# Half of the key projection and the first FFN 2 round on raw, pivot-shifted x in a one-core decoder step

## The chip, the cores and the metric

One core of a Trainium2 chip runs the whole kernel in one launch. The metric is device time in microseconds; lower is better. TensorE is called PE, VectorE DVE, ScalarE ACT, GpSimd POOL and SyncE SP, as in the profile.

## The reference

One layer for 512 prompt tokens and 32 sample tokens (8 sequences of 4), in float32:

```python
x = layer_norm(ALPHA * x + 0.5 * swiglu(x, ffn1_w_gu, ffn1_w_down), ln_g[0], ln_b[0])
qa, ka, va, qr, kr, vr, gr, ga, gb = split(x @ w_in)
oa = diff_post(diff_attention(qa, ka, va))          # paged cache for the sample group
ob = ret_post(retention(qr, kr, vr), gr)
m = sigmoid(ga) * (oa @ w_pa) + sigmoid(gb) * (ob @ w_pb)
x = layer_norm(ALPHA * x + m @ w_o, ln_g[1], ln_b[1])
x = layer_norm(ALPHA * x + 0.5 * swiglu(x, ffn2_w_gu, ffn2_w_down), ln_g[2], ln_b[2])
```

`layer_norm` subtracts the mean over the 1,024 channels, divides by the root of variance + eps, multiplies by a gain and adds a bias, both per channel. `swiglu(x)` is `(silu(a) * u) @ w_down` with `a, u` the halves of `x @ w_gu` (2 x 2,816 columns). The keys `ka` are also an output.

## The kernel before

**Layout.** x stands with channels on partitions: `xT` is 8 channel tiles (KD = 8, index k) of 128 channels x 544 tokens (512 prompt, then 32 sample). Every gemm is a sum of three float32r products, so each operand is split in a high and a low part: `xh`, `xl` for x, `w_hi_t`, `w_lo_t` for weights, `hh`, `hl` for the FFN's hidden tiles, `mh`, `ml` for the merged branches. `gemm` (L289 on) makes one output tile of 128 columns x 544 tokens in two PSUM banks: for each k three products of two halves of 272 tokens, 48 matmuls for 8 k. PSUM has eight banks, so four such tiles.

**Weights.** Chunks of 256 columns (two output tiles) are loaded by SP into one of two `w_raw` buffers, cast by ACT to `w_hi_t` (`split_hi`, once PE is done with the chunk two before) and subtracted by DVE to `w_lo_t` (`split_lo`). PE waits for `lo_split`; SP loads the next chunk into the buffer once the split of the last one there is done.

**Order of work.** Nothing is planned at run time: each engine runs its list of classes in the order in which the blocks at the end of `build` call their `pe_part`, `act_part`, `dve_part` and `pool_part`, and engines meet through semaphores. Around the change the order is: FFN 1 (11 rounds of up chunks, then 12 down chunks), the first channel norm `ln1`, key projection `pk`, value projection, query projection; and much later the output projection `out_proj`, the second channel norm `ln2`, FFN 2 and the last norm `ln3`, which is of another kind and not touched.

**The channel norm** (L571 on). DVE adds each residual tile to `x_sum` as it comes (`dve_add`). After the last one PE sums over partitions with a matrix of ones (L608), DVE centres the eight tiles (L639), ACT squares each (L627) and PE accumulates the squares' sums (L614); ACT takes the root (L629), DVE the reciprocal (L642); then per tile DVE scales (L646), ACT adds the bias twice, into `xh` and `xT` (L633, L634), and DVE makes `xl` (L651). The first gemm behind the norm, tile 0 of `pk` or of FFN 2's first round, waits for each k's `xl` (`ready`).

**Key projection** (`Project`, L660 on). Eight tiles on two pairs of banks. ACT evicts a tile to `turned` (L728), PE transposes it to token rows after the next tile's gemm (`turn`, L699 and L701), DVE copies the rows to `k_nat` (L742, L744), POOL copies the tile to `kaT` (L751).

**FFN** (L315 on). A round makes two tiles of a and two of u in all eight banks: ACT applies silu (L373), DVE multiplies (L394), ACT and DVE split the product. The down projection adds its tiles into `xT` (L413); `out_proj` does the same at L1813.

## Time and profile before

| | |
|---|---|
| median of three timed runs | 1946.93 us (1946.41 to 1950.22) |
| profiled execution: span from its first to its last instruction | 1943.7 us |
| median less that span | 3.2 us |
| PE busy in the span | 1804.9 us, 93% |
| DVE, ACT, POOL busy | 778.9, 667.4, 85.2 us |
| mean granted PE clock | 0.968 of full |

The profile gives the profiled execution's time as its span; what lies around the span is seen only as the distance to the timed runs. The page's 40 slices of 48.6 us show PE at nine tenths or more nearly everywhere; lower are the start, the stretch of the attentions, and single slices near 440 and 1500 us.

### The profile page before, as it was taken

Reading aid. Unit: us, or ns where it says so; the run is one execution under the profiler, and the core shown is the slowest. Engines: PE = TensorE matmul, PEld = TensorE weight load, DVE = VectorE, ACT = ScalarE, POOL = GpSimd, SP = SyncE. Lnnn points to the kernel's source line nnn. Section 1 sums busy time; section 2 is a strip of 40 time slices with the busy share of each in tenths; the row PEclk is TensorE's granted clock in tenths of the full one; section 3 lists DMA queues with packets and bytes.
Section 4 is the critical chain, followed back from the end, with each engine's and each line's share of the span. In section 5 each row is a group of like instructions: output and inputs, shape, how many; then the busy total and the mean of one; then the engine's idle time right before and its main releaser. Section 6 shows DMA issues by size and latency. Waiting matters only on the chain.

```text
span 1943.7 us, 33105 instructions
## 1 busy us (share of the span) xinstructions
PE 1804.9 (93%) x13247; PEld 1699.9 (87%) x13247; DVE 778.9 (40%) x1081; ACT 667.4 (34%) x899; POOL 85.2 (4%) x113
## 2 busy tenths in 40 slices
PE   6999999998997768999989999999999899999996
PEld 5999999987997537878768999869998799999996
DVE  2333332234223875756663223344345433333123
ACT  3333331124223555666563222124322433332111
POOL 0000000000002420000000000110000000000002
PEclk9999999999997998999989999999999999999998
DMA  4222222230440015767752232062223022222221
GB/s 142 91 90 91 89 84 82 81 108 22 133 133 23 1 51 176 273 228 249 242 169 91 87 98 84 17 215 66 91 91 100 22 86 87 89 90 84 92 97 46
DMA packets 146659, 203.75 MB, mean 105 GB/s; under 512 B 5538, under 2 KB 127330, under 8 KB 146594
## 3 DMA queue, kind: packets, MB, share of 16 engines
q1 hardware_dynamic: 145442, 198.35, 31.4%
q0 software_dynamic: 1152, 4.46, 0.6%
q8 instruction: 49, 0.80, 0.2%
q14 instruction: 16, 0.13, 0.0%
HBM read 191.39 MB, written 11.40 MB: 104 GB/s over the span
## 4 chain that ended last, share of the span: by engine, by line
PE 88%; DVE 4%; ACT 4%; issue 2%; DMA 0%; SPq 0%; POOL 0%; ACTq 0%; POOLq 0%; DVEq 0%
PE ps L297 68%; PE ps L1201 4%; PE ps L1232 3%; PE ps L1187 2%; PE ps L974 1%; PE ps L988 1%; PE ps L614 1%; PE ps L1624 1%; PE ps L1211 1%; PE ps L1616 1%; PE ps L1248 1%; PE ps L699 1%; PE ps L1198 1%; ACT aT L1069 1%; PE ps L981 0%
## 5 line engine op out<-in xcount | busy, mean ns | idle before, releaser
L297 PE MATMUL ps<-xh,w_hi_t 128*128 128x272 f32 x2432 | 510.1, 291 | 25.3 <-DVE xl L651 18.3
L297 PE MATMUL ps<-xh,w_lo_t 128*128 128x272 f32 x2432 | 505.9, 290 | 0.0
L297 PE MATMUL ps<-xl,w_hi_t 128*128 128x272 f32 x2432 | 504.2, 289 | 0.0
L283 DVE TENSOR_TENSOR w_lo_t<-w_raw,w_hi_t 128x2048 fp32r<-128x2048 f32 (+1 forms) x112 | 252.4, 2254 | 519.2 <-ACT w_hi_t L279 519.2
L297 PEld LDWEIGHTS ps<-xh,w_hi_t 128*128 128x128 f32 x2432 | 385.0, 190 | 30.2 <-issue 20.7
L297 PEld LDWEIGHTS ps<-xl,w_hi_t 128*128 128x128 f32 x2432 | 385.1, 190 | 0.0
L297 PEld LDWEIGHTS ps<-xh,w_lo_t 128*128 128x128 f32 x2432 | 382.4, 190 | 0.0
L279 ACT CAST w_hi_t<-w_raw 128x2048 fp32r<-128x2048 f32 (+1 forms) x112 | 209.9, 1874 | 276.5 <-PE ps L297 276.5
L297 PE MATMUL ps<-hh,w_lo_t 128*128 128x272 f32 x704 | 145.7, 288 | 0.0
L297 PE MATMUL ps<-hh,w_hi_t 128*128 128x272 f32 x704 | 145.5, 288 | 0.0
L297 PE MATMUL ps<-hl,w_hi_t 128*128 128x272 f32 x704 | 145.1, 288 | 0.0
L297 PEld LDWEIGHTS ps<-hh,w_hi_t 128*128 128x128 f32 x704 | 110.7, 188 | 0.0
L297 PEld LDWEIGHTS ps<-hl,w_hi_t 128*128 128x128 f32 x704 | 110.6, 189 | 0.0
L297 PEld LDWEIGHTS ps<-hh,w_lo_t 128*128 128x128 f32 x704 | 109.9, 189 | 0.0
L1303 DVE TENSOR_TENSOR kt_lo<-ps,kt_hi 128x512 fp32r<-128x512 f32 x128 | 82.5, 685 | 57.3 <-ACT kt_hi L1302 57.1
L377 ACT CAST hh<-prod 128x544 f32 x44 | 28.6, 649 | 216.0 <-DVE prod L394 216.0
L1302 ACT CAST kt_hi<-ps 128x512 fp32r<-128x512 f32 x128 | 70.3, 587 | 66.9 <-PE ps L1187 66.7
L1187 PE MATMUL ps<-ident,k_page 128*128 128x128 f32 x512 | 74.8, 285 | 14.1 <-DVE kt_lo L1303 12.4
L1324 DVE TENSOR_TENSOR vp_lo<-v_page,vp_hi 128x1024 fp32r<-128x1024 f32 x64 | 76.4, 1222 | 19.3 <-ACT vp_hi L1320 18.9
L1187 PEld LDWEIGHTS ps<-ident,k_page 128*128 128x128 f32 x512 | 57.5, 144 | 29.1 <-DVE kt_lo L1303 12.8
L394 DVE TENSOR_TENSOR prod<-ps,gated 128x544 f32<-128x544 f32 x44 | 31.9, 725 | 108.2 <-PE ps L297 108.2
L1201 PE MATMUL ps<-kt_hi,q_stat 128*128 128x256 f32 x256 | 71.9, 314 | 0.0
(245 smaller groups left out, 2107.0 us busy)
## 6 DMA issues: line engine op xcount, KB each, us to landing
w_raw<-in_ffn_w_gu_dram SPq DMA_DIRECT2D x44, 1024.0 KB, 5.1
w_raw<-in_w_in_dram SPq DMA_DIRECT2D x32, 1024.0 KB, 5.7
k_page<-in_cache_k_dram SPq DMA_DIRECT2D x64, 512.0 KB, 4.8
v_page<-in_cache_v_dram SPq DMA_DIRECT2D x64, 512.0 KB, 4.6
w_raw<-in_ffn_w_down_dram SPq DMA_DIRECT2D x16, 1024.0 KB, 5.1
w_raw<-in_ffn_w_down_dram SPq DMA_DIRECT2D x8, 768.0 KB, 4.7
w_raw<-in_w_branch_a_dram SPq DMA_DIRECT2D x4, 1024.0 KB, 5.2
st_in<-in_state_ret_dram SPq DMA_DIRECT2D x8, 512.0 KB, 5.0
```

What stands on the lines that cost most here:

```text
L279: nc.scalar.copy(w_hi_t[:, j, 0:nk], w_raw[:, j, 0:nk]).then_inc(hi_split, 1)
L283: nc.vector.tensor_tensor(w_lo_t[:, j, 0:nk], w_raw[:, j, 0:nk], w_hi_t[:, j, 0:nk].bitcast(F32), ALU.subtract).then_inc(lo_split, 1)
L297: mm = nc.tensor.matmul(ps[:, bank + half, 0:HALF], w[:, j, k, w_cols], m[:, k0 + k, half * HALF:half * HALF + HALF], start=start and k == ...
L377: nc.scalar.copy(hh[:, bass.ds(2 * i + n, 1)], prod[:, n:n + 1]).then_inc(self.h_hi, 1)
L394: nc.vector.tensor_tensor(halves(prod[:, n]), banks(4 + 2 * n), halves(gated[:, n]), ALU.mult).then_inc(self.prod_done, 1)
L614: mm = nc.tensor.matmul(ps[:, 2 + a, 0:HALF], ones[:], x_sq[:, k % 2, a * HALF:a * HALF + HALF], start=k == 0, stop=k == KD - 1)
L1187: mm = nc.tensor.transpose(ps[:, half, h * P:h * P + P], k_page[:, g % 4, (4 * half + h) * P:(4 * half + h) * P + P], ident[:])
L1201: mm = nc.tensor.matmul(dst, q_stat[:, P * h:P * h + P], kt[:, q % 2, h], start=False, stop=h == HA - 1 and kt is kt_lo)
L1232: mm = nc.tensor.matmul(ps[:, 6 + half, :], pT[:, g], v[:, g % 2, 512 * half:512 * half + 512], start=g == 0 and v is vp_hi, stop=False)
L1302: return nc.scalar.copy(at_hi, src)
L1303: return nc.vector.tensor_tensor(at_lo, src, at_hi.bitcast(F32), ALU.subtract)
L1324: nc.vector.tensor_tensor(vp_lo[:, g % 2], v_page[:, g % 4], vp_hi[:, g % 2].bitcast(F32), ALU.subtract).then_inc(self.v_lo, 1)
```

## The change

In both channel norms the gemm behind the norm starts on x that is not yet normalised. With gain g, bias b, mean m and 1/root r per token, `W'((x - m) r g + b) = r (W'(x g) - m W'g) + W'b`. So `xh`, `xl` first hold x times gain, and two more columns (544 becomes 546) hold -g and b; their gemm gives `-W'g` and `W'b` beside the tile. An eviction then computes `(ps + m * fold0) * r` on DVE (`dve_fix`) and adds `fold1` on ACT or in the product. To keep x small, a pivot (the mean over the first two channel tiles) is subtracted early from all eight tiles of `xT` (`dve_pivot`, 8 additions on DVE), while the producer's gemms still run.

- Raw x feeds tiles 0 to 3 of `pk` (all eight came from normalised x) and the whole first round of FFN 2 (four tiles). From tile 4 of `pk` and the second round on, gemms read normalised x.
- Statistics: ACT squares each residual tile, POOL adds the squares into `x_ssq`, and one PE pair per sum gives both sums in the middle of the first raw tile, before k = 5 (`pe_stats`). The variance is the mean square less the squared mean.
- Normalised x: POOL subtracts the mean from the eight tiles, DVE scales, ACT adds the bias and casts to `xh`, DVE makes `xl`; `xh[k]` is overwritten once PE is done with k of the last raw tile (`freed`).
- FFN's down loops, `out_proj` and FFN 2's first round are written out instead of looped. `x_rs`, `x_mu`, `x_msq` and `x_fix` lie in the place of `hh`.

The diff's core (the old bodies of `ChannelNorm` and the key tiles' use of `Project`, printed above, go):

```diff
         xT = at("xT", 49152, [KD, T])
-        xh = at("xh", 66560, [KD, T], F32R)
-        xl = at("xl", 83968, [KD, T], F32R)
-        A = 101376
+        xh = at("xh", 66560, [KD, T + 2], F32R)
+        xl = at("xl", 84032, [KD, T + 2], F32R)
+        A = 101504
...
-        def gemm(bank, j, n, nk, mh_, ml_, k0=0, start=True, stop=True, tile_ready=None):
+        def gemm(bank, j, n, nk, mh_, ml_, k0=0, start=True, stop=True, tile_ready=None, extra=0, freed=None,
+                 between=None):
 
             for k in range(nk):
+                if between and k == 5:
+                    between()
                 if tile_ready:
                     tile_ready(k)
                 w_cols = slice(n * P, n * P + P)
                 for pas, (w, m) in enumerate(((w_hi_t, mh_), (w_hi_t, ml_), (w_lo_t, mh_))):
                     for half in range(2):
-                        mm = nc.tensor.matmul(ps[:, bank + half, 0:HALF], w[:, j, k, w_cols],
-                                              m[:, k0 + k, half * HALF:half * HALF + HALF],
+                        cols = HALF + extra * half
+                        mm = nc.tensor.matmul(ps[:, bank + half, 0:cols], w[:, j, k, w_cols],
+                                              m[:, k0 + k, half * HALF:half * HALF + cols],
                                               start=start and k == 0 and pas == 0,
                                               stop=stop and k == nk - 1 and pas == 2)
+                if freed and k < nk - 1:
+                    mm.then_inc(freed, 1)
             mm.then_inc(gemm_done, 1)
...
+            def pe_stats(self, pe):
+                pe.wait_ge(self.summed, KD * self.i + KD)
+                for a in range(2):
+                    nc.tensor.matmul(ps[:, 4 + a, 0:HALF], ones[:], x_sum[:, a * HALF:a * HALF + HALF],
+                                     start=True, stop=True)
+                pe.wait_ge(self.ssq, KD * self.i + KD)
+                for a in range(2):
+                    mm = nc.tensor.matmul(ps[:, 6 + a, 0:HALF], ones[:], x_ssq[:, a * HALF:a * HALF + HALF],
+                                          start=True, stop=True)
+                mm.then_inc(self.spread, 1)
+
...
+            def act_take(self, act, k, resid, r0):
+                act.wait_ge(resid, r0 + k + 5)
+                act.wait_ge(self.shifted, KD * self.i + KD)
+                act.wait_ge(self.ssq, KD * self.i + k)
+                nc.scalar.activation(x_sq[:], xT[:, k], ACT.Square).then_inc(self.squared, 1)
+                nc.scalar.mul(xh[:, k, 0:T], xT[:, k], self.gain(k)).then_inc(self.raw_hi, 1)
+
+            def act_stats(self, act):
+                act.wait_ge(self.spread, 2 * self.i + 2)
+                nc.scalar.activation(halves(x_msq[:]), banks(4), ACT.Square, scale=1.0 / D).then_inc(self.moment, 1)
+                nc.scalar.mul(halves(x_mu[:]), banks(4), 1.0 / D).then_inc(self.moment, 1)
+                act.wait_ge(self.scale_set, 2 * self.i + 1)
+                nc.scalar.activation(x_rs[:], x_rs[:], ACT.Sqrt, bias=guard[:]).then_inc(self.moment, 1)
+
...
+            def act_high(self, act, k, c):
+                act.wait_ge(self.y, KD * self.i + k + 1)
+                if k < KD - 1:
+                    act.wait_ge(self.freed, (KD - 1) * self.i + k + 1)
+                else:
+                    tile_done(act, c, 1)
+                nc.scalar.copy(xh[:, k, 0:T], xT[:, k]).then_inc(self.y_hi, 1)
+
...
+            def dve_pivot(self, dve):
+                dve.wait_ge(self.kept, 3 * self.i + 3)
+                dve.wait_ge(self.summed, KD * self.i + 1)
+                nc.vector.scalar_tensor_tensor(x_sum[:], x_nc[:], float(self.PIVOT), x_sum[:], ALU.mult, ALU.add
+                                               ).then_inc(self.summed, 1)
+                for k in range(KD):
+                    nc.vector.tensor_tensor(xT[:, k], xT[:, k], x_nc[:], ALU.add).then_inc(self.shifted, 1)
+
...
+                dve.wait_ge(self.shifted, KD * self.i + KD)
+                dve.wait_ge(self.summed, KD * self.i + k)
+                nc.vector.tensor_tensor(x_sum[:], x_sum[:], xT[:, k], ALU.add).then_inc(self.summed, 1)
+                self.dve_raw_low(dve, k)
+
+            def dve_raw_low(self, dve, k):
+                dve.wait_ge(self.raw_hi, KD * self.i + k + 1)
+                nc.vector.scalar_tensor_tensor(xl[:, k, 0:T], xT[:, k], self.gain(k), xh[:, k, 0:T].bitcast(F32),
+                                               ALU.mult, ALU.subtract).then_inc(self.raw_lo, 1)
+
+            def dve_fix(self, dve, u, c, n, bank):
+
+                s = u % 2
+                f = self.f0 + u
+                tile_done(dve, c, n)
+                if u >= 2:
+                    self.fix_free(dve, u)
+                nc.vector.tensor_copy(fold[:, 2 * s:2 * s + 2], ps[:, bank + 1, HALF:HALF + 2]).then_inc(self.fixed, 1)
+                dve.wait_ge(self.fixed, 3 * f + 1)
+                dve.wait_ge(self.moment, 3 * self.i + 2)
+                nc.vector.scalar_tensor_tensor(halves(x_fix[:, s]), halves(x_mu[:]), fold[:, 2 * s:2 * s + 1], banks(bank),
+                                               ALU.mult, ALU.add).then_inc(self.fixed, 1)
+                dve.wait_ge(self.fixed, 3 * f + 2)
+                nc.vector.tensor_tensor(x_fix[:, s], x_fix[:, s], x_rs[:], ALU.mult).then_inc(self.fixed, 1)
+
+            def dve_scale(self, dve, k):
+                dve.wait_ge(self.centered, KD * self.i + k + 1)
+                nc.vector.scalar_tensor_tensor(xT[:, k], xT[:, k], self.gain(k), x_rs[:], ALU.mult, ALU.mult
+                                               ).then_inc(self.scaled, 1)
+
+            def dve_low(self, dve, k):
+                dve.wait_ge(self.y_hi, KD * self.i + k + 1)
+                nc.vector.tensor_tensor(xl[:, k, 0:T], xT[:, k], xh[:, k, 0:T].bitcast(F32), ALU.subtract
+                                        ).then_inc(self.x_lo, 1)
+
+            def pool_part(self, pool):
+                for k in range(KD):
+                    pool.wait_ge(self.squared, KD * self.i + k + 1)
+                    if k == 0:
+                        nc.gpsimd.tensor_copy(x_ssq[:], x_sq[:]).then_inc(self.ssq, 1)
+                    else:
+                        pool.wait_ge(self.ssq, KD * self.i + k)
+                        nc.gpsimd.tensor_tensor(x_ssq[:], x_ssq[:], x_sq[:], ALU.add).then_inc(self.ssq, 1)
+                pool.wait_ge(self.moment, 3 * self.i + 2)
+                pool.wait_ge(self.raw_lo, (KD + 2) * (self.i + 1))
+                for k in range(KD):
+                    nc.gpsimd.tensor_tensor(xT[:, k], xT[:, k], x_mu[:], ALU.subtract).then_inc(self.centered, 1)
...
+        class NormedProject(Project):
+            RAW = 4
...
+            def pe_part(self, pe):
+                for u in range(self.tiles):
+                    if u % 2 == 0:
+                        chunk_ready(pe, self.c + u // 2)
+                    pe.wait_ge(self.taken, self.t0 + u + 1)
+                    ready = {0: lambda k: self.norm.raw_ready(pe, k), self.RAW: lambda k: self.norm.ready(pe, k)}.get(u)
+                    gemm(2 * (u % 2), (u // 2) % 2, u % 2, KD, xh, xl, tile_ready=ready, extra=2 if u < self.RAW else 0,
+                         freed=self.norm.freed if u == self.RAW - 1 else None,
+                         between=None if u else lambda: self.norm.pe_stats(pe))
+                    if u > 0:
+                        self.turn(pe, u - 1)
+
+            def act_part(self, act):
+                self.norm.act_stats(act)
+                for u in range(self.tiles):
+                    if u == self.RAW - 1:
+                        for k in range(KD):
+                            self.norm.act_high(act, k, self.c + u // 2)
+                    s = u % 2
+                    if u < self.RAW:
+                        act.wait_ge(self.norm.fixed, 3 * (self.norm.f0 + u) + 3)
+                    else:
+                        tile_done(act, self.c + u // 2, s)
+                    act.wait_ge(self.rows, self.r0 + u + 1)
+                    act.wait_ge(self.kept, self.k0 + u + 1)
+                    if u < self.RAW:
+                        nc.scalar.activation(self.stage[:, s], x_fix[:, s], ACT.Identity, bias=fold[:, 2 * s + 1:2 * s + 2]
+                                             ).then_inc(self.taken, 1)
+                    else:
+                        nc.scalar.copy(halves(self.stage[:, s]), banks(2 * s)).then_inc(self.taken, 1)
+                    if u % 2 == 1:
+                        c = self.c + u // 2 + 2
+                        split_hi(act, c, c // 2, (u // 2) % 2)
+                    if u < self.RAW - 1:
+                        for k in range(3 * u, min(3 * u + 3, KD)):
+                            self.norm.act_bias(act, k)
...
+                self.norm.dve_stats(dve)
+                for u in range(self.tiles):
+                    if u == self.RAW - 1:
+                        for k in range(KD):
+                            self.norm.dve_low(dve, k)
+                    if u < self.RAW:
+                        self.norm.dve_fix(dve, u, self.c + u // 2, u % 2, 2 * (u % 2))
+                    if u:
+                        keep(u - 1)
+                    if u % 2 == 1:
+                        split_lo(dve, self.c + u // 2 + 2, (u // 2) % 2)
+                    if u < self.RAW - 1:
+                        for k in range(3 * u, min(3 * u + 3, KD)):
+                            self.norm.dve_scale(dve, k)
+                keep(self.tiles - 1)
...
+                if folded:
                     for n in range(2):
+                        folded.dve_fix(dve, n, c, n, 2 * n)
+                split_lo(dve, c + 2 * i + 2, 0)
+                if folded:
+                    for k in range(KD):
+                        folded.dve_scale(dve, k)
+                for n in range(2):
+                    if folded:
+                        folded.dve_fix(dve, 2 + n, c + 1, n, 4 + 2 * n)
+                    else:
                         tile_done(dve, c + 2 * i + 1, n)
...
+                    if folded and n == 0:
+                        for k in range(KD):
+                            folded.dve_low(dve, k)
+                split_lo(dve, c + 2 * i + 3, 1)
...
+                for k in range(KD):
+                    c = self.c + k // 2
+                    tile_done(dve, c, k % 2)
+                    if k > 2:
+                        ln2.dve_shifted(dve)
+                    nc.vector.scalar_tensor_tensor(halves(xT[:, k]), banks(2 * (k % 4)), 1.0 / ALPHA, halves(xT[:, k]),
+                                                   ALU.mult, ALU.add).then_inc(self.resid, 1)
+                    if k == 2:
+                        dve.wait_ge(self.resid, k + 5)
+                        ln2.dve_pivot(dve)
+                        ln2.dve_raw_low(dve, 0)
+                        ln2.dve_raw_low(dve, 1)
+                    ln2.dve_take(dve, k, self.resid, 0)
+                    if k % 2 == 1:
+                        split_lo(dve, c + 2, k // 2 % 2)
+                ln2.dve_stats(dve)
```

In FFN 1's last down chunk ACT casts the next weight chunk and then takes tiles 6 and 7 (`act_take`); DVE's order there and at two other places is shown below. How instructions move:

DVE, from the last residual tiles of FFN 1 on, before (`L413` residual, `L603` running sum, `L283` weight split, `L639` centring, `L646` scale):

```order
L413 SCALAR_TENSOR_TENSOR xT<-ps,xT 128x544 x2
L603 TENSOR_TENSOR x_sum<-x_sum,xT 128x544 x2
L283 TENSOR_TENSOR w_lo_t<-w_raw,w_hi_t 128x2048
L639 SCALAR_TENSOR_TENSOR xT<-ps,xT 128x544 x8
L642 RECIPROCAL x_rs<-x_rs 128x544
L646 SCALAR_TENSOR_TENSOR xT<-xT,ln_cols,x_rs 128x544 x2
L651 TENSOR_TENSOR xl<-xT,xh 128x544
```

The same place now (`L796` sum, `L801` raw split, `L806` variance, `L819` to `L825` the fix of tile 0, `L829` scale):

```order
L493 SCALAR_TENSOR_TENSOR xT<-ps,xT 128x544 x2
L796 TENSOR_TENSOR x_sum<-x_sum,xT 128x544
L801 SCALAR_TENSOR_TENSOR xl<-xT,ln_cols,xh 128x544
L796 TENSOR_TENSOR x_sum<-x_sum,xT 128x544
L801 SCALAR_TENSOR_TENSOR xl<-xT,ln_cols,xh 128x544
L289 TENSOR_TENSOR w_lo_t<-w_raw,w_hi_t 128x2048
L806 SCALAR_TENSOR_TENSOR x_rs<-ps,x_msq 128x544
L809 RECIPROCAL x_rs<-x_rs 128x544
L819 COPY small<-ps 128x2
L822 SCALAR_TENSOR_TENSOR x_fix<-x_mu,small,ps 128x544
L825 TENSOR_TENSOR x_fix<-x_fix,x_rs 128x544
L829 SCALAR_TENSOR_TENSOR xT<-xT,ln_cols,x_rs 128x544 x3
```

The raw splits stand between the sums and the weight split moved behind them; the reciprocal is followed by a tile's fix before the first scale.

PE, between the last down gemm and the first key tile, before:

```order
L297 MATMUL ps<-hl,w_hi_t 128x272 x2
L297 MATMUL ps<-hh,w_lo_t 128x272 x2
L355 REGISTER_ALU
L355 COMPARE_AND_BRANCH
L608 MATMUL ps<-x_sum,ones 128x272 x2
L614 MATMUL ps<-x_sq,ones 128x272 x16
L297 MATMUL ps<-xh,w_hi_t 128x272 x2
L297 MATMUL ps<-xl,w_hi_t 128x272 x2
```

PE inside the first key tile now, from its channel 4 to its channel 5:

```order
L307 MATMUL ps<-xl,w_hi_t 128x272
L307 MATMUL ps<-xl,w_hi_t 128x274
L307 MATMUL ps<-xh,w_lo_t 128x272
L307 MATMUL ps<-xh,w_lo_t 128x274
L716 MATMUL ps<-x_sum,ones 128x272 x2
L720 MATMUL ps<-x_ssq,ones 128x272 x2
L307 MATMUL ps<-xh,w_hi_t 128x272
L307 MATMUL ps<-xh,w_hi_t 128x274
```

The sums moved from ahead of the first tile into it, and the 16 square-sum matmuls became two.

POOL, its first work of the kernel, before (copies of evicted key tiles):

```order
L2087 UNCONDITIONAL_BRANCH
L748 UNCONDITIONAL_BRANCH
L748 ISA
L751 ISA
L751 COPY kaT<-turned 128x544
```

And now, the squares' sums and the eight subtractions ahead of the same copies:

```order
L2361 UNCONDITIONAL_BRANCH
L841 COPY x_ssq<-x_sq 128x544
L844 ISA
L844 TENSOR_TENSOR x_ssq<-x_ssq,x_sq 128x544 x7
L848 TENSOR_TENSOR xT<-xT,x_mu 128x544 x8
L938 UNCONDITIONAL_BRANCH
L938 ISA
L941 ISA
L941 COPY kaT<-turned 128x544
```

The key copies stand behind sixteen operations that wait for ACT and DVE.

## Rows read from the trace of the kernel before

**Rows 1.** The page's chain that ended last: shares of the span by engine.

```profile
PE 88%; DVE 4%; ACT 4%; issue 2%; DMA 0%; SPq 0%; POOL 0%; ACTq 0%; POOLq 0%; DVEq 0%
```

**Rows 2.** Windows: stretch, length; busy (count) of PE, PEld, DVE, ACT, POOL; clock; DMA.

```profile
426.40:460.00 33.60, 19.88 (x79) 15.45 (x79) 24.08 (x29) 20.15 (x28) 0.00 (x0) 0.80 0.11 34
460.00:500.00 40.00, 40.00 (x323) 39.94 (x324) 11.26 (x13) 9.21 (x10) 3.85 (x6) 1.00 0.20 58
1496.50:1530.00 33.50, 20.46 (x84) 15.28 (x84) 23.53 (x28) 20.16 (x28) 0.00 (x0) 0.80 0.10 32
```

**Rows 3.** Timeline, first norm: start, length, engine, line, operation, [idle before <-releaser].

```profile
425.72 0.41 PE L297 MATMUL ps<-hl,w_hi_t 128*128 128x272 f32 x2
...
425.98 0.41 PE L297 MATMUL ps<-hh,w_lo_t 128*128 128x272 f32 x2
...
428.67 1.19 PE L608 MATMUL ps<-x_sum,ones 128*128 128x272 f32 x4 [2.28 <-DVE x_sum L603]
...
430.73 5.13 DVE L639 SCALAR_TENSOR_TENSOR xT<-ps,xT 128x544 f32<-128x544 f32 x8
...
450.03 0.79 PE L297 MATMUL ps<-xh,w_hi_t 128*128 128x272 f32 x2 [7.49 <-DVE xl L651]
...
460.75 0.42 PE L297 MATMUL ps<-xh,w_hi_t 128*128 128x272 f32 x2
```

**Rows 4.** Chain in order of time, key projection: start, length, what.

```profile
480.61 6.01 PE ps L297 x48
...
487.16 6.01 PE ps L297 x48
```

**Rows 5.** Timeline, second norm, TensorE.

```profile
1496.20 0.41 PE L297 MATMUL ps<-mh,w_lo_t 128*128 128x272 f32 x2
...
1530.15 0.41 PE L297 MATMUL ps<-xh,w_hi_t 128*128 128x272 f32 x2
```

**Rows 6.** Groups of VectorE by line and form: busy, mean ns, idle before.

```profile
L283 DVE TENSOR_TENSOR w_lo_t<-w_raw,w_hi_t 128x2048 fp32r<-128x2048 f32 x104 | 238.4, 2292 | 448.2 <-ACT w_hi_t L279 448.2
...
L646 DVE SCALAR_TENSOR_TENSOR xT<-xT,ln_cols,x_rs 128x544 f32<-128x544 f32 x16 | 12.3, 779 | 0.1
...
L642 DVE RECIPROCAL x_rs<-x_rs 128x544 f32<-128x544 f32 x2 | 7.1, 3553 | 14.3 <-ACT x_rs L629 14.3
```

**Rows 7.** Groups of ScalarE by line and form.

```profile
L279 ACT CAST w_hi_t<-w_raw 128x2048 fp32r<-128x2048 f32 x104 | 198.0, 1904 | 198.2 <-PE ps L297 198.2
...
L633 ACT ACTIVATE xh<-xT,ln_cols 128x544 fp32r<-128x544 f32 x16 | 12.0, 748 | 9.9 <-DVE xT L646 9.9
...
L627 ACT ACTIVATE x_sq<-xT 128x544 f32<-128x544 f32 x16 | 10.5, 657 | 11.6 <-PE ps L614 8.5 <-DVE xT L639 3.1
```

**Rows 8.** Groups of GpSimd by line and form.

```profile
L568 POOL TENSOR_TENSOR xn<-xn,ln_bias 128x1024 f32<-128x1024 f32 x4 | 9.4, 2345 | 639.8 <-ACT xn L508 639.8
...
L1691 POOL TENSOR_TENSOR qx<-qrT,cross 128x512 f32<-128x512 f32 x3 | 3.8, 1269 | 6.2 <-PE ps L1587 3.8 <-PE ps L1584 2.4
```

**Rows 9.** Timeline, start of the attention, VectorE and GpSimd.

```profile
610.57 2.29 DVE L283 TENSOR_TENSOR w_lo_t<-w_raw,w_hi_t 128x2048 fp32r<-128x2048 f32 x1 [9.72 <-ACT w_hi_t L279]
...
610.95 2.17 POOL L958 TENSOR_TENSOR bias<-dist,small 128x128 f32<-128x128 f32 x1 [1.16 <-DVEq L1101]
...
614.08 0.28 DVE L1020 CUSTOM_DVE_ANT_0 s_sb<-ps,bias 128x128 f32<-128x128 f32 x1
...
615.02 0.39 POOL L958 TENSOR_TENSOR bias<-dist,small 128x128 f32<-128x128 f32 x1
```

**Rows 10.** Windows behind the two idle stretches; columns as above, clock in the eighth.

```profile
450.00:452.00 2.00, 1.97 (x9) 2.00 (x10) 1.91 (x3) 1.79 (x4) 0.00 (x0) 0.50 0.00 0
...
454.00:456.00 2.00, 1.52 (x11) 1.29 (x10) 1.87 (x4) 2.00 (x4) 0.00 (x0) 0.94 0.00 0
1498.40:1500.50 2.10, 1.91 (x4) 0.96 (x4) 1.92 (x1) 1.63 (x3) 0.00 (x0) 0.57 0.00 0
```

**Rows 11.** The page's costliest group: busy, mean ns of one, idle before.

```profile
L297 PE MATMUL ps<-xh,w_hi_t 128*128 128x272 f32 x2432 | 510.1, 291 | 25.3 <-DVE xl L651 18.3
```

More of the change, by code:

```diff
@@ L379, in act_part @@
+            def act_part(self, act, folded=None, norm=None):
+                c = self.c
+                if folded:
+                    self.act_up(act, 0, folded)
+                with act.Fori(1 if folded else 0, KF // 2) as i:
+                    self.act_up(act, i)
                 c += FFN_UP
+                if norm:
+                    norm.act_columns(act)
                 for q in range(2):
@@ L384, in act_part @@
                             split_hi(act, c + nxt, (c + nxt) // 2, m % 2, 6 if m % 3 == 0 else KD)
-            def dve_part(self, dve, norm=None):
+                        if norm and q == 0 and m == 3:
+                            norm.act_pivot(act)
+                            for k in range(2):
+                                norm.act_take(act, k, self.resid, self.r0)
+                        if norm and m % 3 == 2 and (q, m) != (0, 2):
+                            for k in (4 * q + 2 * (m // 3), 4 * q + 2 * (m // 3) + 1):
+                                norm.act_take(act, k, self.resid, self.r0)
@@ L609, in pe_part @@
                                           start=True, stop=True)
-                mm.then_inc(self.mean, 1)
-                for k in range(KD):
-                    pe.wait_ge(self.squared, KD * self.i + k + 1)
-                    for a in range(2):
-                        mm = nc.tensor.matmul(ps[:, 2 + a, 0:HALF], ones[:], x_sq[:, k % 2, a * HALF:a * HALF + HALF],
-                                              start=k == 0, stop=k == KD - 1)
-                    mm.then_inc(self.sq_used, 1)
@@ L2044, in _ @@
             pe.wait_ge(cols_set, 1)
[L2045 to L2047 removed]
+            ffn1.pe_part(pe, norm=ln1)
+            pk.pe_part(pe)
             pv.pe_part(pe, before=pk)
```

328 lines of the change are left out of this document (198 added, 130 removed).

## Prediction

> **What bounds the kernel now.** I read the chain of waits first: 88% of it is TensorE (PE), so time is won only where PE stands or works in vain [rows 1]. Then the windows, for where that is: in an ordinary stretch PE is busy all the time (40.00 of 40.00 us), but in the two stretches that hold the channel layer norms it is busy for 19.88 of 33.60 and 20.46 of 33.50 us, and much of that is norm work, at a mean clock of 0.80 [rows 2]. Then the timeline, for what those stretches cost. At the first norm the last pair of FFN 1 matmuls starts at 425.98 and the second key tile at 460.75 [rows 3]. A pair starts every 0.25 us and a tile of 48 matmuls takes 6.02 [rows 4], so between these two points only 0.25 + 6.02 are gemm: 34.77 - 6.27 = **28.5 us** are lost. At the second norm the same two points are 1496.20 and 1530.15 [rows 5]: 33.95 - 6.27 = **27.7 us**. Together 56.2 us, 2.9% of the span of 1943.7. That is all there is to win, and the change must give some of it back.
>
> **What it removes.** The chain sum - mean - eight centrings - eight squares - square root - reciprocal - scale - split no longer stands between the last residual tile and the first matmul. The raw tiles of channels 0 to 5 are split while the producer's gemms still run; PE goes on with them at once. The eight square-sum pairs on PE vanish too, but they lie inside the 56.2 us.
>
> **What it adds on PE.** Per norm: one pair of ones-matmuls for the pivot and two for the statistics. The pair of today takes 1.19 us to its end [rows 3]; an end stands 0.16 behind the next start (0.41 against 0.25 [rows 3, 4]), so I take 1.03. Six pairs: **6.2 us**, all in PE's own queue. The two more columns on half of the matmuls of eight tiles are 2 in 272 of 0.125 us, under 0.2 us in all: left out.
>
> **What it adds on VectorE (DVE), ScalarE (ACT) and GpSimd (POOL).** Durations of 128x544 operations: DVE 0.72, next start after 0.64 (eight in 5.13 [rows 3]); scale or split of raw x with a gain column 0.78, weight split 2.29, reciprocal 3.55 [rows 6]; ACT square 0.66, cast with gain 0.75, weight cast 1.90 [rows 7]. POOL's two-input operation has no row of this size: 512 columns take 1.27, 1,024 take 2.35 [rows 8], so a line through both gives 1.34 for 544. A key-tile fix is three DVE operations that wait for one another: 0.2 + 0.8 + 0.8, about 1.8.
>
> One row pattern decides the sum. A POOL operation that takes 0.39 alone took 2.17 when it was issued 0.38 us behind a weight split on DVE, and ended 0.26 behind it; a DVE operation with one operand in PSUM took its usual 0.28 while POOL ran [rows 9]. I read this as: a DVE instruction with both inputs in SBUF and a POOL instruction hold each other up, whole instruction by whole instruction. The new kernel puts sixteen POOL operations per norm beside just such DVE work: the squares' sum beside raw splits, the eight subtractions (10.7 us in a row) beside fix, scale and weight split.
>
> **First norm, step by step** (us from the last FFN 1 matmul; every engine works in the order of its code):
> - PE does channels 0 to 4 of tile 0 until 3.8, then must have the full sum. DVE takes channel 7's residual (0.2), the sum of channel 6 (0.8), then the raw split of 6. That needs ACT, which first casts a weight chunk (to 2.1), squares (to 2.8) and casts (to 3.5); and POOL adds square 6 until 4.1. So the last sum is ready at 5.6, square sums 0.3 later: **2.2 idle**.
> - Statistics, variance behind a weight split (9.8 on), root, reciprocal until 14.9, fix of tile 0 held once by POOL: evicted at 17.9. PE finished tile 1 at 16.0 and waits to transpose tile 0: **1.9**.
> - DVE's scale 0 to 2 each stand behind one subtraction, so the fix of tile 1 is late: **1.2**. Tile 2's fix stands behind the weight split and scale 3 to 5: **2.1**.
> - Scale 6 and 7, their biases, then the first normalised split: ready at 38.6, PE free at 34.9: **3.7**. After that a split each 0.66 keeps ahead of PE's 0.75 per channel.
> - Tile 3's fix stands behind all eight splits: **0.9**. From there on the spacing is 6.56 as before [rows 4].
> Idle: 12.0 us.
>
> **Second norm** (us from the first out-projection matmul): pivot sum on PE at 18.1, negated mean 19.8, eight shifts until 25.7, then raw splits 0 to 3 in turn with POOL's additions; ACT's weight cast stands behind them (34.6), DVE's split ends at 38.9 where PE wanted it at 37.1: **1.9**. The statistics cost no wait here, as residuals come every 6 us. In the first FFN 2 round the fixes, the weight split and eight scales end at 78.1, then fix 2, the product, its cast, and only then the normalised splits: first at 82.8, where PE is free at 76.9: **5.9**. Idle: 7.8 us.
>
> **The clock.** [...] Four microseconds at half clock lose about 1.8 of work. I charge it twice, behind the 3.7 and the 5.9: **3.6 us**.
>
> **Sum.** 12.0 + 7.8 + 6.2 + 3.6 = 29.6 us stay; 56.2 - 29.6 = 26.6 are won. The sum is made against a profile whose span is 1943.7; the median of the runs shown, 1946.93, stands 3.2 above it, and I keep that distance: 1946.9 - 26.6 = **1920**. Hidden at no cost: the pivot's eight shifts in FFN 1's down projection (5.9 us of DVE, beside a chunk of 9 to 12 us whose weight split has some 6 to spare), the new columns (cut while that stage begins), POOL's shifts of its key copies. If that cover went, a weight split would be late and PE would wait for it, as I count for the out projection. Loads follow the weight splits on SP's queue and shift with them by 2 us at most, with a chunk's time to spare. The PE loops that are written out cost nothing: the key tiles are written out today and run at 6.02 us [rows 4].
>
> [...]
>
> **Rivals.**
> - *POOL and DVE hardly meet.* For: the episode is one, and POOL's other rows keep their length. Against: that episode has both sides of it. Without any hold the same count gives 5.8 + 5.6 of idle: 11.4 + 6.2 + 3.6 = 21.2 stay, 35.0 won, **1912**; 1908 if the clock does not fall either. Chance 0.20.
> - *A heavier POOL or more waits.* At 1.8 us per POOL operation idle is 15.6 + 13.3 and the time 1929; at 2.35 (the row of 1,024 columns, the upper bound) 1941. For: the squares' sum adds in place, which no row does at this size. Against: the rows of 1.27 hardly scatter. Chance 0.20 for 1925 to 1942.
> - *Slower: the subtractions on POOL set the order.* Everything normalised hangs on them, one after another. Above 2.6 us each the idle exceeds 46 us and the gain is gone; at 3.5 it is 31 + 39 and the time about 1970. Nothing in [rows 8] is near. The same sign would come from the new row length of xh and xl, 546 columns instead of 544, if it slowed the reads: no row shows such a stride, so its cost lies between nothing and unknown; 3 times 2,432 matmuls read them [rows 11], 7.3 us per nanosecond each, so 3.6 ns (of 125) would eat the gain. I take nothing, as the rows of hh and xh run alike. Chance 0.04.
> - *It does not do what it says:* raw tiles might still wait for the statistics. They don't by the code: only channels 5 to 7 of the first tile stand behind them. 0.01.
>
> **How the numbers follow.** Forecast 0.55 (1914 to 1925), rivals 0.20, 0.20, 0.05. The range of 1907 to 1932 takes in the forecast, the first rival and the nearer half of the second. What a measurement of this kernel can tell from no change is about 0.2%, 4 us: faster 0.93 (all but the far end of the second rival and the last two), same 0.03, slower 0.04.
>
> **What would show it.** Of the 56 us lost at the two norms about 30 should be left; the stats pair should start about 5.6 us behind the last FFN 1 matmul; PE should wait for splits of normalised x by about 4 and 6 us, clock 0.5 after it; POOL's subtractions should stretch beyond 1.34 where DVE scales, and DVE's scales beyond 0.78. Right, but for other reasons: idle of 11 us and unstretched rows. Wrong: subtractions above 2 us, gemms of xh slower than 6.02 per tile, or late weight splits in the down projection.

## The result and the profile after

The changed kernel takes 1933.84 us (median of 4 runs, 1932.99 to 1937.74) against 1948.58 for the kernel before in the same comparison (1946.41 to 1951.81): a ratio of 0.9923, 95% interval 0.9906 to 0.994. The medians differ by 14.7 us; the interval of the ratio makes that 11.7 to 18.3. It is faster, as forecast, but by about half of the 26.6 us, and 1934 lies above the range. A second comparison gave 1933.52 against 1948.56 and 0.9925 (0.9906 to 0.9944). The profiled execution has a span of 1935.7 and a time of 1937.74, the longest of its four runs.

The chain of waits on the page of the changed kernel, which answers to [rows 1]:

```profile
PE 85%; DVE 6%; ACT 5%; issue 3%; DMA 0%; SPq 0%; POOL 0%; ACTq 0%; POOLq 0%; DVEq 0%
```

TensorE still sets the end. Now the stretch that held the first norm, for TensorE, in order of time (start, length, engine, line, operation, idle before with its releaser); it answers to [rows 3]:

```profile
431.84 0.41 PE L307 MATMUL ps<-hh,w_lo_t 128*128 128x272 f32 x2
432.09 0.42 PE L307 MATMUL ps<-xh,w_hi_t 128*128 128x272 f32 x2
...
437.53 1.18 PE L716 MATMUL ps<-x_sum,ones 128*128 128x272 f32 x4 [1.45 <-DVE x_sum L796]
438.72 1.19 PE L720 MATMUL ps<-x_ssq,ones 128*128 128x272 f32 x4
...
449.39 0.66 PE L889 MATMUL ps<-ident,turned 128*128 128x128 f32 x4 [1.10 <-ACT turned L984]
...
456.43 0.66 PE L889 MATMUL ps<-ident,turned 128*128 128x128 f32 x4 [0.17 <-ACT turned L984]
...
465.07 0.66 PE L889 MATMUL ps<-ident,turned 128*128 128x128 f32 x4 [1.78 <-ACT turned L984]
...
468.63 0.79 PE L307 MATMUL ps<-xh,w_hi_t 128*128 128x272 f32 x2 [2.79 <-DVE xl L834]
```

The first key tile starts 0.25 us behind the last FFN 1 matmul, where it stood 24 us behind it before. What is left of the gap lies in five waits: for the full sum (1.45), for three evicted tiles at their transposition (1.10, 0.17, 1.78) and for normalised xl ahead of tile 4 (2.79). The groups of TensorE's waits around the second norm (what waited, for whom, us in total, times, longest):

```profile
PE ps L307 <- DVE xl L834: 4.9, 1, 4.9
PE ps L307 <- DVE w_lo_t L289: 1.6, 1, 1.6
```

From the last FFN 1 matmul to the eviction of the eighth key tile the kernel before needed 80.5 us and this one 65.5. From the last out-projection matmul to the end it was 447.5 and is 432.0. These are 15.0 and 15.5 us won, so the mechanism works. The evictions of the eighth key tile, before and after (start, length, engine, line, operation); they stand 80.50 us behind 425.98 of [rows 3] and 65.53 behind 431.84 above:

```profile
506.48 0.62 ACT L728 ACTIVATE turned<-ps 128x544 f32<-128x544 f32 x1 [5.94 <-PE ps L297]
```

```profile
497.37 0.61 ACT L987 COPY turned<-ps 128x544 f32<-128x544 f32 x1 [6.02 <-PE ps L307]
```

What ate into it is seen outside the norms. The chain in order of time, for key and value tiles of the changed kernel (start, length, what, matmuls), which answers to [rows 4]:

```profile
497.88 6.06 PE ps L307 x48
504.49 6.09 PE ps L307 x48
511.13 6.06 PE ps L307 x48
```

A tile of the same 48 matmuls took 6.01 before. The gate and up projections of FFN 1 show it best, as nothing else stands between their tiles: from the first silu of one weight pair to that of the next lie four tiles. Two neighbouring ones before, then two after:

```profile
133.13 0.62 ACT L373 ACTIVATE gated<-ps 128x544 f32<-128x544 f32 x1
...
157.19 0.62 ACT L373 ACTIVATE gated<-ps 128x544 f32<-128x544 f32 x1
```

```profile
135.90 0.63 ACT L406 ACTIVATE gated<-ps 128x544 f32<-128x544 f32 x1
...
160.28 0.63 ACT L406 ACTIVATE gated<-ps 128x544 f32<-128x544 f32 x1
```

Over ten such steps the mean is 24.05 us before and 24.37 after: 6.013 us a tile against 6.093. FFN 2 shows the same two steps behind its first two rounds. The projections of raw x are only eight of the 152 tiles that read xh and xl, but FFN 1, far ahead of them, is slower as well. At the price of FFN 1 that is 152 x 0.080 = **12.2 us** (an estimate: the tiles of other stages were not timed one by one).

### The profile page after: what moved, and what is told of

It reads as the page before. It is cut to its first block, busy times and chain, and to the rows that moved or that the text cites. A ratio compares the mean times of both kernels' runs of the same rounds, so it can differ in the third digit from the quotient of the medians.

```text
span 1935.7 us, 32971 instructions
## 1 busy us (share of the span) xinstructions
PE 1808.8 (93%) x13199; PEld 1707.9 (88%) x13199; DVE 817.8 (42%) x1125; ACT 667.3 (34%) x915; POOL 136.5 (7%) x145
## 4 chain that ended last, share of the span: by engine, by line
PE 85%; DVE 6%; ACT 5%; issue 3%; DMA 0%; SPq 0%; POOL 0%; ACTq 0%; POOLq 0%; DVEq 0%
PE ps L307 65%; PE ps L1462 4%; PE ps L1493 3%; PE ps L1448 3%; PE ps L1235 2%; PE ps L1249 1%; PE ps L1877 1%; PE ps L1885 1%; PE ps L1509 1%; PE ps L1472 1%; ACT w_hi_t L285 1%; PE ps L1459 1%; PE ps L889 1%; DVE small L1125 1%; ACT aT L1330 1%
## 5 line engine op out<-in xcount | busy, mean ns | idle before, releaser
L307 PE MATMUL ps<-xh,w_hi_t 128*128 128x272 f32 (+1 forms) x2432 | 515.9, 293 | 14.5 <-DVE xl L834 7.7
L307 PE MATMUL ps<-xl,w_hi_t 128*128 128x272 f32 (+1 forms) x2432 | 510.1, 291 | 0.0
L307 PE MATMUL ps<-xh,w_lo_t 128*128 128x272 f32 (+1 forms) x2432 | 509.6, 291 | 0.0
L307 PEld LDWEIGHTS ps<-xh,w_hi_t 128*128 128x128 f32 x2432 | 389.0, 192 | 16.8 <-issue 13.0
L307 PEld LDWEIGHTS ps<-xh,w_lo_t 128*128 128x128 f32 x2432 | 389.0, 191 | 0.0
L413 ACT CAST hh<-prod 128x544 f32 (+1 forms) x44 | 28.5, 648 | 215.4 <-DVE prod L461 209.6
```

The costliest lines, as they stand in the source:

```text
L307: mm = nc.tensor.matmul(ps[:, bank + half, 0:cols], w[:, j, k, w_cols], m[:, k0 + k, half * HALF:half * HALF + cols], start=start and k == ...
L413: nc.scalar.copy(hh[:, bass.ds(2 * i + n, 1)], prod[:, n:n + 1]).then_inc(self.h_hi, 1)
```

## The experiments

**What slows the tiles.** The change makes a row of xh and xl 546 columns of 4 bytes long, 2184 bytes. The old rows, 2176 bytes, all start at a multiple of 64 bytes, the new ones at every multiple of 8. Five runs ask whether it is the length, the start, or something else in the new kernel. To make room, the addresses behind xl move and one small tile of 32 columns shares its place with another that is out of use by then; nothing else changes.

The kernel before with longer rows (`b_546`):

```diff
-xh = at("xh", 66560, [KD, T], F32R)
-xl = at("xl", 83968, [KD, T], F32R)
+xh = at("xh", 66560, [KD, T + 2], F32R)
+xl = at("xl", 84032, [KD, T + 2], F32R)
```

> The kernel before with nothing changed but the row length of xh and xl, 546 columns in place of 544 (two columns of each row are never read). Theory (the start of a row decides: rows 2184 bytes apart start at every multiple of 8 bytes): FFN 1 runs a tile of 48 matmuls in 6.09 us in place of 6.01, as the changed kernel does, the key tiles come every 6.63 in place of 6.56, and with 152 tiles that read xh the time is 1947 + 152 x 0.08 = 1959. Rival (the pace of the changed kernel comes from something else in it: the written-out round, the longer kernel, POOL's work): 6.01 a tile and 1947.

Measured: 1958.31 against 1948.95, ratio 1.0053 (1.0035 to 1.0071): by the ratio 10.3 us more (6.8 to 13.8). Its chain shows the tiles of the changed kernel:

```profile
497.62 6.06 PE ps L297 x48
504.23 6.09 PE ps L297 x48
```

So two columns that nobody reads, in a kernel that has none of the new norm, cost what the changed kernel pays: FFN 1's tiles take 6.093, as there. The rival, another cause in the new code, is out.

The same rows of 544 columns, started later (`b_off8`, `b_off32`, `b_off16`; 2, 8 and 4 columns, xl alike):

```diff
-xh = at("xh", 66560, [KD, T], F32R)
+xh = at("xh", 66560, [KD * T + 16], F32R)[:, 2:2 + KD * T].rearrange("p (k t) -> p k t", t=T)
```

> The kernel before, rows of xh and xl again 544 columns apart, but both tensors start 8 bytes later, so that every row starts 8 bytes behind a multiple of 64. Theory (the start of a row decides): slower tiles, 0.08 to 0.09 us each, 6.09 to 6.11, and 1959 to 1961. Rival (the distance between rows, 546 columns, decides): 6.01 a tile and 1947.

> As the run with 8 bytes, but both tensors start 32 bytes later. If a row must start at a multiple of 64 bytes: 6.09 to 6.11 us a tile and 1959 to 1961. If a multiple of 32 or less is enough: 6.01 and 1947.

> The kernel before with both tensors 16 bytes later, all rows 16 bytes behind a multiple of 64. From the rows of 548 columns (starts 0, 16, 32 and 48, twice each), which cost 0.013 us a tile, and the start at 32, which cost nothing: between 0.01 and 0.03 us a tile, 6.02 to 6.04, if the cost of an odd start is that of the place within 32 bytes; 6.01 if only multiples of 16 count; 6.09 or more if nothing short of 32 helps.

Measured: 1970.04 us (8 bytes), 1952.77 (32 bytes) and 1954.98 (16 bytes), one run each, beside 1948.95, 1948.95 and 1948.56. The tiles tell it without the scatter of single runs (chains of the three in this order):

```profile
501.66 6.16 PE ps L297 x48
...
508.36 6.14 PE ps L297 x48
```

```profile
507.54 6.01 PE ps L297 x48
```

```profile
502.41 6.03 PE ps L297 x48
...
508.99 6.01 PE ps L297 x48
```

In FFN 1 a tile takes 6.160, 6.013 and 6.027 us. With all rows 8 bytes off, each matmul is 3.06 ns longer (0.147 / 48), about twice the 1.66 that rows of 546 columns cost in the mean; 152 x 0.147 = 22.3 us agrees with the 21 measured. I had expected 0.08 to 0.09 a tile there: the eight starts of the 546-column rows are not equally dear. At 32 bytes the cost is gone, at 16 nearly; the run at 32 also has the moved addresses of the others, so these cost nothing. The row length is out, and the start decides. It also accounts for the 546 columns: half of their rows start off a multiple of 16, and if each of those costs what a start at 8 costs, the mean is 0.147 / 2 = 0.074 a tile of the 0.080 measured (an estimate; starts at 24, 40 and 56 were not run singly).

The changed kernel with rows of 548 columns (`a_548`):

```diff
-xh = at("xh", 66560, [KD, T + 2], F32R)
-xl = at("xl", 84032, [KD, T + 2], F32R)
+xh = at("xh", 66560, [KD, T + 4], F32R)
+xl = at("xl", 84096, [KD, T + 4], F32R)
```

> The changed kernel with rows of 548 columns for xh and xl, 2192 bytes, so that every row starts at a multiple of 16 bytes (one eighth of them at 0, 16, 32, 48 twice each modulo 64). Theory (start of a row) if a multiple of 16 is enough: 6.01 us a tile, 152 x 0.08 = 12 us less, 1922, close to what was forecast. Theory if a multiple of 64 is needed: six rows of eight are still off it, about 6.08 a tile and 1932. Rival (rows don't matter): 6.09 and 1934.

Measured: 1926.33 against 1948.95, ratio 0.9873 (0.9852 to 0.9893): by the ratio 24.7 us less than before (20.8 to 28.8). Tiles take 6.027 in FFN 1:

```profile
499.43 6.03 PE ps L307 x48
506.00 6.04 PE ps L307 x48
```

Against the changed kernel's 0.9923 that is 0.0050, or 9.7 us; 152 x (6.093 - 6.027) = 10.0 us. Most of the gain that was missing comes back with two more unused columns. The norms themselves are as they were: waits of 7.3 us at the first and 6.8 at the second.

**What VectorE's and GpSimd's hold costs.** Groups by line and form of the changed kernel (busy, mean ns, idle before), and four rows of its timeline:

```profile
L801 DVE SCALAR_TENSOR_TENSOR xl<-xT,ln_cols,xh 128x544 fp32r<-128x544 f32 x16 | 18.6, 1160 | 9.9 <-ACT xh L746 9.9
L829 DVE SCALAR_TENSOR_TENSOR xT<-xT,ln_cols,x_rs 128x544 f32<-128x544 f32 x16 | 14.8, 983 | 0.0
L822 DVE SCALAR_TENSOR_TENSOR x_fix<-x_mu,small,ps 128x544 f32<-128x544 f32 x8 | 6.2, 780 | 0.3
L848 POOL TENSOR_TENSOR xT<-xT,x_mu 128x544 f32<-128x544 f32 x16 | 23.8, 1526 | 6.2 <-ACT x_mu L751 6.2
L844 POOL TENSOR_TENSOR x_ssq<-x_ssq,x_sq 128x544 f32<-128x544 f32 x14 | 23.2, 1655 | 87.7 <-ACT x_sq L745 87.7
```

```profile
441.16 12.21 POOL L848 TENSOR_TENSOR xT<-xT,x_mu 128x544 f32<-128x544 f32 x8 [2.49 <-ACT x_mu L751]
...
442.90 3.56 DVE L809 RECIPROCAL x_rs<-x_rs 128x544 f32<-128x544 f32 x1 [0.82 <-ACT x_rs L753]
...
448.48 5.47 DVE L829 SCALAR_TENSOR_TENSOR xT<-xT,ln_cols,x_rs 128x544 f32<-128x544 f32 x3
...
478.25 1.74 POOL L941 COPY kaT<-turned 128x544 f32 x1 [2.07 <-ACT turned L987]
```

The raw split (two operands in SBUF) takes 1.16 in the mean in place of the 0.78 of [rows 6]: the group mixes six of 0.77 to 0.78 with ten of 1.34 to 1.57 that meet GpSimd's additions. The first three scales take 5.47, the next three, behind the last subtraction, 2.17. The fix with an operand in PSUM keeps its 0.78 beside the subtractions, the reciprocal with one input its 3.56 (3.55 in [rows 6]). So the hold is there, and in these rows only VectorE's instructions with both inputs in SBUF feel it. One run takes the subtractions away, and their hold with them (`a_548_nosub`, on `a_548`; it leaves the centring of normalised x out):

```diff
-nc.gpsimd.tensor_tensor(xT[:, k], xT[:, k], x_mu[:], ALU.subtract)
+nc.gpsimd.tensor_tensor(xT[:, k, 0:1], xT[:, k, 0:1], x_mu[:, 0:1], ALU.subtract)
```

> The changed kernel with rows of 548 columns; POOL subtracts the mean from one column of each channel in place of 544, so the normalised x stays uncentred: this work is left out. Theory of the forecast (VectorE's scales are held by the subtractions, and PE's waits at the norms come from that): scales fall from 1.82 to 0.7 us, and PE's idle at the first norm from 7.3 to 4 or less. Rival (the hold is there, but most of PE's waits stand behind other work: sums, weight splits, the order): scales fall as well, but PE's idle at both norms stays within 2 us of 14.

Measured: 1920.64 in one run (before 1954.62). VectorE's three scales:

```profile
445.19 2.55 DVE L829 SCALAR_TENSOR_TENSOR xT<-xT,ln_cols,x_rs 128x544 f32<-128x544 f32 x3
```

TensorE's waits at the first norm fall from 7.3 to 4.7 (1.5, 0.9 and 2.4), those at the second stay (4.9 and 1.6). Neither expectation holds whole: the 4 us of the first is missed by little, and the sum of both norms falls by 2.7, not by at most 2. The size is the result: the hold by the subtractions costs about 2.5 us of waits, all at the first norm. Forecast and the rival without any hold stood 8.4 apart, but that rival also lets go of the squares' additions, which are kept here: the two last raw splits still take 1.34 and 1.55.

**What can be won at the norms.** Six raw key tiles (`a_548_raw6`), and normalised splits earlier in FFN 2 (`a_548_n2`), apart and together (`a_best`), on `a_548`:

```diff
-RAW = 4
+RAW = 6
...
-ln1 = ChannelNorm(0, 4)
+ln1 = ChannelNorm(0, 6)
```

```diff
                     for k in range(KD):
                         folded.act_bias(act, k)
+                        if k:
+                            folded.act_high(act, k - 1, c + 1)
+                    folded.act_high(act, KD - 1, c + 1)
...
                     for k in range(KD):
                         folded.dve_scale(dve, k)
+                    for k in range(KD):
+                        folded.dve_low(dve, k)
```

(the same calls further down are taken out).

> The changed kernel with rows of 548 columns, and six in place of four raw key tiles. Theory (the wait for normalised splits of 2.6 us ahead of tile 4 and the half clock behind it, 8.8 in place of 6.0 us for that tile, are a matter of too little cover; two more raw tiles give 13 us of it): both go, 5.3 us less than the same kernel with four, about 1921; two more fixes on DVE find room. Rival (DVE is the bound there and the wait moves): the later fixes and the splits push PE's turns or tile 6 back by as much, 1925 to 1927.

> The changed kernel with rows of 548 columns; in the first FFN 2 round the eight normalised splits stand ahead of the fix of tile 2 and of the cast of its product, ACT's bias and cast taking turns channel by channel. Theory (the wait of 5.1 us at the second round is the order on DVE and ACT, and costs half a clock of 2.7 behind it): the wait falls to about 1 us, the clock holds, 6 to 7 us less than the same kernel without it, about 1920. Rival (the products, now 5 us later, hold PE up in place of the splits): same time, 1925 to 1927.

> Rows of 548 columns, six raw key tiles and the early normalised splits of FFN 2 together. Theory: both savings add, 1926 - 5.3 - 6.7 = 1914. Rival (either moves its wait): 1920 or more.

Measured, beside a kernel before at 1954.62 in this comparison: 1921.49, ratio 0.9828 (0.9811 to 0.9845); 1926.22, 0.9858 (0.9838 to 0.9878); 1920.58, 0.9819 (0.9797 to 0.9841). The kernel before was 6 us slower in this comparison than beside `a_548`, so the times decide nothing between theory and rival: for all together the time is the rival's 1920, and the ratio, 0.9819 of 1948.95, the theory's 1914. The stages in the traces part them: with both edits they give 3.6 us, not 12. Six raw tiles: from the last FFN 1 matmul to the eighth key eviction 61.3 in place of 64.4, 3.1 won of the 5.3 expected (64.4 is `a_548`). The wait ahead of the normalised tile is gone, but the clock still falls, now behind the 1.83 us wait for tile 2 (windows of `a_548_raw6`; columns as in [rows 2]):

```profile
460.00:462.00 2.00, 0.21 (x2) 0.00 (x0) 1.97 (x5) 1.08 (x2) 0.00 (x0) 1.00 1.00 327
462.00:464.00 2.00, 1.96 (x12) 1.96 (x13) 1.97 (x4) 1.29 (x2) 1.73 (x1) 0.71 0.11 38
464.00:466.00 2.00, 2.00 (x11) 2.00 (x10) 1.77 (x4) 1.10 (x3) 0.03 (x1) 0.50 0.00 0
466.00:468.00 2.00, 2.00 (x17) 2.00 (x16) 0.37 (x1) 1.60 (x1) 0.61 (x1) 0.94 0.00 0
```

The early splits alone win nothing that shows: from the last out-projection matmul to the end 429.4 in place of 429.9. Here the rival is right that the wait moves, though not to the products. TensorE's timeline:

```profile
1520.09 0.49 PE L307 MATMUL ps<-xh,w_hi_t 128*128 128x272 f32 x2 [1.16 <-DVE xl L833]
...
1536.35 0.54 PE L307 MATMUL ps<-xh,w_hi_t 128*128 128x272 f32 x2 [3.98 <-DVE w_lo_t L289]
```

The wait of 5.1 us became 1.16 for the splits and 3.98 for the second weight split, whose cast stands on ScalarE behind the products' casts. The last version (`a_best2`) on `a_best` puts that weight chunk first:

```diff
                     folded.act_high(act, KD - 1, c + 1)
+                    split_hi(act, c + 2 * i + 3, c // 2 + i + 1, 1)
                 for n in range(2):
...
-                    dve.wait_ge(self.h_hi, self.h0 + 2 * i + n + 1)
-                    nc.vector.tensor_tensor(hl[...], prod[:, n:n + 1], hh[...].bitcast(F32), ALU.subtract)
                 split_lo(dve, c + 2 * i + 3, 1)
+                if folded:
+                    for n in range(2):
+                        self.dve_hidden(dve, i, n)
+                    dve.wait_ge(self.h_lo, self.h0 + 2)
```

> As the kernel with 548 columns, six raw key tiles and early normalised splits, and in the first FFN 2 round the second weight chunk's cast stands ahead of the casts of the products, its split ahead of the products' low parts. Theory (the 4.0 us that PE waited there for the weight split came from these operations queued ahead of it): the wait falls under 1 us and the kernel takes 3 to 4 us less, a ratio to the kernel before of about 0.980 in place of 0.982. Rival (VectorE is full in this round, so the split can't end earlier): still 3 us or more of wait in all, ratio 0.982.

Measured: **1912.20** against 1948.56, ratio 0.981 (0.9794 to 0.9827). The one wait that is left in this round:

```profile
1513.37 0.49 PE L307 MATMUL ps<-xh,w_hi_t 128*128 128x272 f32 x2 [1.14 <-DVE xl L843]
```

The 3.98 for the weight split are gone, so VectorE was not full; what is left misses "under 1 us" by little. From the last out-projection matmul to the end 423.8 us, 5.6 less than `a_best` (429.4) in the traces, where 3 to 4 were expected. The two ratios' intervals overlap, so the runs alone don't part these two; `a_best2` lies clear below the changed kernel and the kernel before.

**Two stages that the change doesn't touch.** In the first profile after, the last pages of the decode attention (from its last score matmul to the sum of its outputs) took 41.6 us in place of 37.2, and the retention's sample steps 33.1 in place of 28.2. The second of these in the timeline of the changed kernel (groups of eight matmuls of one line, 3.77 us long in the slow part and 1.99 behind it) and in its windows, where the granted clock, in the eighth place, is 0.50:

```profile
1268.40 3.77 PE L1885 MATMUL ps<-vr_nat_s,kw_s 32*128 32x256 f32 x8
...
1279.77 1.99 PE L1885 MATMUL ps<-vr_nat_s,kw_s 32*128 32x256 f32 x8
```

```profile
1270.00:1275.00 5.00, 5.00 (x13) 2.40 (x12) 1.41 (x4) 0.00 (x0) 1.03 (x1) 0.50 0.08 30
```

> The changed kernel as it is, profiled a second time. Two stages that the change does not touch were longer in its first profile than in that of the kernel before: the last pages of the decode attention by 4.4 us and the retention's sample steps by 4.9, each with TensorE at a granted clock of 0.5. If that is chance of the single execution, the second profile shows other lengths (37 to 41 and 28 to 33 us). If the change brings it about, they are 41.4 and 33.1 again.

Measured: 41.4 and 28.2 us. The decode stage was 41.4 again, but by its length it belongs to neither kernel: in the traces of the five kernels with the code of before it lies between 37.2 and 41.5 (41.5 in `b_off16` and `b_off32`), in the eight with that of the changed kernel between 37.3 (`a_best2`) and 41.6. That is chance of the execution, with the profile of the kernel before at the short end. The sample steps came out short in one execution of the changed kernel and long in another, so the change alone doesn't bring them about. That it has no part in them is not shown: the long form stands again in `a_548` and `a_best2`, three of the eight, and in none of the five.

## Why the prediction was wrong

Step by step, in us that stay at the norms or are added, forecast against the profile after:

| term | forecast | measured |
|---|---|---|
| waits, first norm | 12.0 | 7.3 |
| waits, second norm | 7.8 | 6.5 |
| six pairs with ones | 6.2 | 5.7 |
| half clock | 3.6 | 4.8 |
| row starts of xh and xl | 0 | 12.2 (estimate) |
| sum | 29.6 | 36.5 |

**The step that failed** is the sentence on the new row length, "I take nothing, as the rows of hh and xh run alike". The rows were right and proved nothing: both tensors had rows of 544 columns, all at multiples of 64 bytes, so no row of either showed what a start off such a place costs. The rival was named, with the count (7,296 matmuls, 7.3 us for each nanosecond) and the point at which it would turn the sign (3.6 ns), but not given a middle: 1.66 ns were measured, and nothing in the range stood for it. Its own sign of being wrong, "gemms of xh slower than 6.02 per tile", is the one that came. Without that term the changed kernel would stand at 1933.8 - 12.2 = 1921.6 (an estimate), near the 1920 forecast; with most of it taken away `a_548` measured 1926.3.

That closeness is not all merit. By the table 56.2 - 36.5 = 19.7 us should have been won, and the interval of the runs reaches from 11.7 to 18.3; `a_548` shows the same gap (19.7 + 10.0 against 24.7, 20.8 to 28.8). So the waits that came out 6.0 us below the forecast were made up for elsewhere, by some 5 us. The traces show where, though not why. Leave out the stages that the change works in (the down projection of FFN 1, the key tiles, the out projection, FFN 2 up to its down projection) and take off what the slower tiles cost in the rest: 1390 to 1398 us remain in the five traces with the code of before (mean 1393.9), 1394 to 1402 in the eight of the changed code (mean 1399.0). Nearly 3 of the 5 us lie in the decode attention, from its first score matmul to the first gemm behind it. Single traces of the two overlap, so whether the change brings this about or the executions scatter stays open. The forecast had no term for it.

**Waits, first norm.** The order of events was right: the pair for the sum starts 5.69 us behind the last FFN 1 matmul (forecast 5.6), then wait by wait 1.45, 1.10, 0.17, 1.78, 2.79 and nothing for 2.2, 1.9, 1.2, 2.1, 3.7 and 0.9. Two things made them shorter than forecast. TensorE came to them later than counted: at 4.2 us for the sum where 3.8 was taken, at 16.5 for the first evicted tile where 16.0 was. And the hold was counted as whole instructions standing behind one another, a scale behind a whole subtraction. In the rows three scales took 5.47, 1.82 each and 1.04 above their own 0.78, not 1.34 above it, and the first four subtractions, beside the variance and the one-input reciprocal, followed one another every 1.36 (441.16 to 446.59). So the first normalised split was ready at 36.8 us in place of 38.6. How much of each wait is due to which of the two was not separated.

On VectorE's side the hold reached only instructions with both inputs in SBUF in these rows. Beside the subtractions the reciprocal, with one input, kept its 3.56 and the fix's first step, with one operand in PSUM, its 0.78, while its product, with both inputs in SBUF, took 1.06 in place of 0.72 and three scales 1.82 each. The forecast counted the reciprocal as free of the hold, though [rows 9] has no one-input instruction beside GpSimd's work; that was an assumption of mine. On GpSimd's side a one-input copy to `kaT` took 1.74 at 478.25, beside VectorE's weight split, in place of the 0.64 of the copy at 475.54.

**Second norm.** 1.63 and 4.87 for 1.9 and 5.9, in the two places named. **Ones.** A pair took 0.92 to the next start at the second norm, two together 2.01 at the first. **Clock.** The forecast of 3.6 us rests on [rows 10]. The clock fell to 0.50 at the two places named, behind 2.79 and 4.87 us, for 2.8 and 2.0 us of lost work; windows of the first norm:

```profile
468.00:470.00 2.00, 1.37 (x6) 1.40 (x7) 2.00 (x4) 2.00 (x5) 0.00 (x0) 0.50 0.00 0
470.00:472.00 2.00, 2.00 (x11) 2.00 (x11) 2.00 (x4) 1.56 (x3) 0.00 (x0) 0.50 0.00 0
472.00:474.00 2.00, 2.00 (x11) 2.00 (x11) 1.93 (x5) 0.00 (x0) 0.00 (x0) 0.50 0.00 0
474.00:476.00 2.00, 2.00 (x16) 2.00 (x16) 1.37 (x3) 1.38 (x2) 0.46 (x1) 0.93 0.00 0
```

**The rivals.** No hold: the rows refute it, though the hold is worth less than the 8.4 us between the two: 2.5 of waits go with the subtractions. A heavier POOL: its means of 1.53 and 1.65 lie near the 1.8 of that rival, but they mix. Where VectorE runs nothing with both inputs in SBUF, an operation takes 1.35 to 1.39, near the 1.34 of the forecast; the longer ones stand beside such an instruction, with 1.82 to 1.85 beside scales and fixes and 2.91 beside a weight split. The waits did not grow either. Slower by the subtractions: none is near 2.6 us. Slower by the row length: the right sign, at half of the price at which it eats the gain; it is where the rows start, not how long they are: rows of 544 columns took 6.160 us a tile with starts 8 bytes off (`b_off8`) and 6.013 at 32 (`b_off32`).

## What to carry to other kernels

When a change lengthens the rows of an operand that TensorE streams, look at where each row starts before looking at the new work: here two columns cost 10 us in `b_546`, and rows of 548 in place of 546 gave as much back. A comparison of two rows of a trace says something of a price only if they differ in the thing that is priced. After removing one wait at a norm, follow the same engine's queue to the next transfer or split that it delays, as the early splits here moved 4 of their 5 us onto a weight split.

## What was not expected of the hardware

In FFN 1, whose matmuls stream 272 four-byte columns, a matmul took 3.06 ns more with rows 8 bytes behind a multiple of 64 (`b_off8`: 6.160 us a tile against 6.013), 0.28 more at 16 bytes (`b_off16`: 6.027), and no more at 32 (`b_off32`: 6.013). The starts of 546-column rows cost 1.66 in the mean (`b_546`: 6.093). Starts at other places were not tried singly, nor other column types.

The clock fell behind shorter waits than the two that the forecast charged it to: behind the 1.83 us for tile 2 in `a_548_raw6` it stood at 0.71 and 0.50 for the next four microseconds, while it had stayed at 1.00 behind the 1.14 and 0.23 us before. [rows 10] had shown the same, 0.57 behind an idle of some 2 us.
